# Second attention on one core: the order of product kinds alternates from step to step on TensorE, ScalarE and VectorE, and opening banks are exchanged

## The chip, the cores and the metric

The kernel runs on one core of a Trainium2 chip. The metric is the device time of one execution in microseconds; lower is better. The kernel before takes 1789.56 us, the median of three runs (1787.97 to 1791.72).

The core's engines are named as the profile names them: PE is TensorE (matmuls; PEld its weight loads), DVE is VectorE, ACT is ScalarE, POOL is GpSimd, SP is SyncE, which issues the transfers. Each works through its own list of instructions in order, and they wait for each other by semaphores.

## What is computed

Two transformer blocks for one sequence of 512 tokens and width 1024, all in float32. The first has a feed-forward layer, a Fourier mixer with latent attention, and another feed-forward layer. The second block has an attention of two kinds and a feed-forward layer. The change lies in the attention of the second block:

```python
NSA_HEADS = 8
NSA_KV = 2
DSA_HEADS = 8
DSA_TOPK = 256
...
o_nsa = nsa_attention(...)   # compressed, selected and windowed branches, gated by g
    o = g[..., 0:1] * o_cmp + g[..., 1:2] * o_slc + g[..., 2:3] * o_win
...
o_dsa = dsa_attention(...)   # keys chosen by an index score
        _, sel = lax.top_k(score, k_top)
        s = jnp.einsum('bqhd,bqkd->bhqk', qg, kg) * scale
        p = masked_softmax(s, mask)
...
        o = jnp.concatenate([o_nsa, o_dsa], axis=-1) @ w_out[l]
```

With 512 tokens the selected and the windowed branch see all earlier keys, so each of the 8 NSA heads has two causal softmaxes over up to 512 keys (one with the keys `ks`, one with `kw`) beside a small one over the compressed keys. The 8 DSA heads have one each, over keys `kd`, with a mask made from the 128 best index scores of a row.

## The kernel before

The order of all work is written out by hand, engine by engine; every wait is a semaphore. Activations lie transposed (features on partitions, 512 tokens along the free axis). Weights come in through `raw`, GpSimd splits each into a high and a low part, and three float32r products make one float32 product (`mm3`, lines 768 to 770). These products fill most of the span.

The second attention stands between the projections and the output product. Its work is cut into 12 pairs of heads, `PAIRS`: 8 for the NSA branches (for each of four head numbers one with `ks` and one with `kw`, two heads side by side) and 4 for DSA. A pair has 4 steps, one for each 128 queries; step s of a pair (s % 4 = 0 to 3) has 128, 256, 384 or 512 keys, since later keys are masked. Of each step, on each engine:

- TensorE, `pair_scores(s)` (line 1378): two score products of 64 rows each, side by side on the array, into two of the four banks `B_S2`. It waits until VectorE has read the scores of step s - 2 (`at_nm`).
- VectorE, `pair_maxima` (line 2529): adds the mask to the scores in PSUM, writes them to `p2` and takes the row maximum, `at_nm`.
- ScalarE, `pair_exp` (line 1895): the exponential with its row sum, in place, `at_exp`.
- VectorE, `pair_inverse(s)` (line 2537), one step later: the reciprocal of two row sums, `pr_inv`.
- GpSimd, `scale_probabilities` (line 745): times the reciprocal (and the gate), `pr_p`. In the first steps pieces of two weight splits stand between.
- TensorE, `pair_transposes(s)` (line 1389), `LAG_T` = 3 steps after the scores: 1 to 4 blocks of 128 x 128 for each of two heads, into the two banks `B_T2`. A transpose waits until its bank was copied out (`at_ev`).
- ScalarE, `pair_turn` (line 1890): copies the turned blocks from PSUM to `pt2`, `at_ev`.
- TensorE, `pair_values` (line 1409), `LAG_V` = 7 steps after the scores: the products with the values, step j of a pair with 512 - 128 j columns, side by side for two heads, into a bank of `B_O`. The first of a pair waits for the copies of the whole pair:

```python
            if j == 0:
                pe.wait_ge(at_ev, PAIR_T0 + 8 * pi + 8)
```

For every second NSA pair two products of the compressed branch (`compressed_values`, line 1394) stand ahead of them. Where a chunk of the output ends, ScalarE copies it out (line 1902) and VectorE takes the low part (line 2552). On VectorE `select(1)` stands beside steps 4 to 31 (three steps of four): one round of the choice of the best index scores (lines 2408 and 2409).

In each step TensorE has scores, transposes, values in this order; ScalarE has the copies of step s - 3 and then the exponentials of step s; VectorE has the maxima first. Ahead of step 1 TensorE turns the probabilities of the compressed branch (`turn_compressed`, line 1421), into banks 4 and 6, and waits until ScalarE has copied them to `ptc` (line 1882), since bank 4 is also one of the scores'. `rotate2(13)`, the last rotation of the queries `qd`, is done by VectorE in step 1 (lines 2260 to 2263) from data which ScalarE copies (`raw_copy(13)`).

Of the kernel before, what the change touches and what calls it, by code (L numbers as in the profile page):

```python
# [16 lines left out]
F32 = mybir.dt.float32  # L17
# [6 lines left out]
P = 128  # L24
D = 1024
T = 512
# [112 lines left out]
def build(nc, a, out):  # L139
# [514 lines left out]
    MLA_STEPS = 2 * MLA_HEADS  # L654
    LAG_T1, LAG_V1 = 2, 3
    B_S, B_T, B_O = (0, 1, 2, 4), (3, 5), (6, 7)
    B_S2, B_T2 = (1, 5, 4, 0), (2, 3)
    def turned1(t):

        return (sq, tt)[t // 2 % 2][:, t % 2]  # L660
# [105 lines left out]
    def _(pe):  # L766
# [605 lines left out]
        def pair_scores(s):  # L1372
            for t in (2 * s, 2 * s + 1):
                if t >= 4:
                    pe.wait_ge(at_nm, PAIR_T0 + t - 3)
            w = P * (s % 4 + 1)
            for side, x in enumerate(PAIRS[s // 4]):
                pe.matmul(ps[:, B_S2[(2 * s + side) % 4], 0:w], x["q"](s % 4), x["k"](w),  # L1378
                          start=True, stop=True).then_inc(at_s, 1)

        def pair_transposes(s):
            for t in (2 * s, 2 * s + 1):
                pe.wait_ge(pr_p, t + 1)
                if t < 2:
                    pe.wait_ge(rp_out, ROT1 + 14)
                else:
                    pe.wait_ge(at_ev, PAIR_T0 + t - 1)
                for c in range(s % 4 + 1):
                    last = pe.transpose(ps[:, B_T2[t % 2], P * c:P * c + P], p2[:, (t + 4) % P_SLOTS, P * c:P * c + P], ident)  # L1389
                last.then_inc(at_tr, 1)  # L1390

        def compressed_values(c):
            for g in range(NSA_KV):
                pe.matmul(ps[HD * g:HD * g + HD, B_O[c % 2]], v_diag[:, g, c, :], ptc[:, g, :], start=True, stop=False)

        def pair_values(pi, j):

            c = chunk_of(pi)
            if j == 0:
                pe.wait_ge(at_ev, PAIR_T0 + 8 * pi + 8)  # L1400
                if pi >= 8 or pi % 2 == 0:
                    if c >= 2:
                        pe.wait_ge(o_lo_done, PAIR_C0 + c - 1)
                    if pi == 0:
                        pe.wait_ge(cm_kv_ev, 2)
                    if pi < 8:
                        compressed_values(c)
            for side, x in enumerate(PAIRS[pi]):
                last = pe.matmul(ps[HD * side:HD * side + HD, B_O[c % 2], P * j:T], x["v"](j),  # L1409
                                 turned(8 * pi + side)(PT_ROW * j + P * j, T - P * j),  # L1410
                                 start=pi >= 8 and j == 0, stop=chunk_ends(pi) and j == 3)
            if j == 3:
                last.then_inc(pr_pv, 1)

        def turn_compressed():
            pe.wait_ge(cm_sub, 2)
            for b in range(2):
                pe.wait_ge(cm_p, b + 1)
                for gr in range(2):
                    for q in range(2):  # L1420
                        last = pe.transpose(ps[:, 4 + 2 * b, P * (2 * gr + q):P * (2 * gr + q) + P],
                                            cs[:, b, P * (2 * q + gr):P * (2 * q + gr) + P], ident)
                last.then_inc(cm_tr, 1)

        pe.wait_ge(rp_rot, ROT1 + 13)
        pe.wait_ge(cm_hid_ev, 2)
        for s in range(PAIR_STEPS + LAG_V + 1):
            if s == 1:
                turn_compressed()
                pe.wait_ge(cm_ev, 2)  # L1430
                pe.wait_ge(rp_rot, ROT1 + 14)
            if s == 32:
                pe.wait_ge(kd_up, 1)
            if s < PAIR_STEPS:
                pair_scores(s)
            if LAG_T <= s < PAIR_STEPS + LAG_T:
                pair_transposes(s - LAG_T)
            pi, j = values_at(s)
            if pi is not None:
                pair_values(pi, j)  # L1440

        pe.wait_ge(o_lo_done, 12)
        for i in range(8):
# [137 lines left out]
    def _(act):  # L1581
# [295 lines left out]
            act.activation(cs[:, b], cs[:, b], ACT.Exp, scale=HD ** -0.5).then_inc(cm_exp, 1)  # L1877
        raw_copy(12)
        raw_copy(13)
        for b in range(2):  # L1880
            act.wait_ge(cm_tr, b + 1)
            act.copy(ptc[:, :, 2 * P * b:2 * P * b + 2 * P],
                     ps[:, 4 + 2 * b].rearrange("p (g q) -> p g q", g=2)).then_inc(cm_ev, 1)
# [13 lines left out]

        for s in range(PAIR_STEPS + LAG_V + 1):
            c = finished_at(s)
            if c is not None:  # L1900
                act.wait_ge(pr_pv, (s - LAG_V) // 4)
                act.copy(h_hi[:, c], ps[:, B_O[c % 2]]).then_inc(o_hi_done, 1)
            for t in (2 * (s - LAG_T), 2 * (s - LAG_T) + 1):
                if 0 <= t < 2 * PAIR_STEPS:
                    pair_turn(t)
            for t in (2 * s, 2 * s + 1):
                if t < 2 * PAIR_STEPS:
                    pair_exp(t)

        root_table(act)  # L1910
        norm_squares(act, 4, y_ready, 0, y2)
# [20 lines left out]
    def _(dve):  # L1932
# [600 lines left out]
        def pair_inverse(s):  # L2533
# [2 lines left out]
            c = 2 * s % 16  # L2536
            dve.reciprocal(small2[:, 32 + c:34 + c], small2[:, 16 + c:18 + c]).then_inc(pr_inv, 1)

        rotate2(12, qd[:, 2])
        values_diagonal()  # L2540
        for s in range(PAIR_STEPS + LAG_V + 1):
            for t in (2 * s, 2 * s + 1):
                if t < 2 * PAIR_STEPS:
                    pair_maxima(t)
            if 1 <= s <= PAIR_STEPS:
                pair_inverse(s - 1)
            if s == 1:
                rotate2(13, qd[:, 3])
            c = finished_at(s)
            if c is not None:  # L2550
                dve.wait_ge(o_hi_done, PAIR_C0 + c + 1)
                dve.tensor_tensor(h_lo[:, c], ps[:, B_O[c % 2]], h_hi[:, c].bitcast(F32), ALU.subtract).then_inc(o_lo_done, 1)  # L2552
            if 4 <= s < 32 and s % 4 < 3:
                select(1)

        step(dve.tensor_tensor(postmix2, fac[:, A_POSTMIX:A_POSTMIX + 8], fac[:, A_POSTMIX:A_POSTMIX + 8], ALU.mult))
        def out2(m):
# [139 lines left out]
```

## Time and profile before

| | us |
|---|---|
| median of three runs | 1789.56 |
| lowest and highest run | 1787.97, 1791.72 |
| the profiled execution, its own time | 1787.86 |
| its span in the trace | 1786.1 |
| TensorE busy in the span | 1763.6 (99%) |
| GpSimd, VectorE, ScalarE busy | 1181.0 (66%), 974.3 (55%), 382.4 (21%) |
| the second attention, first score product to first output product | 1248.1 to 1363.6 |
| TensorE busy in these 115.6 us | 109.4 |
| VectorE, ScalarE, GpSimd busy in them | 83.3, 95.9, 69.4 |

The span is what the trace shows of one execution; the time of the execution is 1.8 us longer. Busy shares are means over the stretch. PEclk is the granted clock of TensorE as a share of the full 2.4 GHz; 0.50 is the lower level of 1.2 GHz. A row's idle time is the engine's time without work just before it, with the instruction that ended it.

### The profile page before, as it was taken

The page shows a single profiled execution, that of the slowest core. Times are in us where ns is not written, and L with a number is a line of the kernel's source. Part 1 is how long each engine was busy: PE and PEld are TensorE (multiplying, and loading weights), DVE is VectorE, ACT ScalarE, POOL GpSimd, SP SyncE. Part 2 cuts the span into 40 slices and gives each one's busy share as a digit, 9 for nine tenths or more (in the row PEclk, how much of TensorE's full clock was granted, in tenths as well). Part 3 has the DMA queues.
Part 4 walks back from the last instruction along what each step waited for, and adds up shares of the span by engine and source line. Part 5 has one row for each costly group of instructions (what it writes and reads, how often), then busy time and mean ns, then how long its engine had stood idle before and what let it go on. Part 6 is the DMA issues. An engine that isn't in the chain of part 4 may idle for free.

```text
span 1786.1 us, 24918 instructions
## 1 busy us (share of the span) xinstructions
PE 1763.6 (99%) x8821; PEld 1394.4 (78%) x8821; DVE 974.3 (55%) x1664; ACT 382.4 (21%) x827; POOL 1181.0 (66%) x1182
## 2 busy tenths in 40 slices
PE   8999999999999999999999999999999999999998
PEld 6888888887876788888888888878446778888887
DVE  4855345544655105565514556799874887007613
ACT  3111000012246211211100001455884110000001
POOL 4676767675665477677677768755754677668862
PEclk9999999999999999999999999999999999999999
DMA  9655465542330132455435543513000322333221
GB/s 355 215 189 176 141 206 186 161 153 66 100 99 25 36 107 94 142 171 188 125 110 191 188 127 94 127 50 95 25 25 1 95 71 96 114 96 93 95 94 48
DMA packets 245549, 212.93 MB, mean 119 GB/s; under 512 B 45986, under 2 KB 240991, under 8 KB 245471
## 3 DMA queue, kind: packets, MB, share of 16 engines
q1 hardware_dynamic: 229440, 211.18, 37.0%
q10 hardware_dynamic: 16030, 0.72, 0.5%
q8 instruction: 48, 0.79, 0.2%
q14 instruction: 31, 0.25, 0.0%
HBM read 209.72 MB, written 2.10 MB: 119 GB/s over the span
## 4 chain that ended last, share of the span: by engine, by line
PE 70%; POOL 13%; issue 9%; DVE 5%; DMA 1%; ACT 1%; ACTq 0%; POOLq 0%; DVEq 0%
PE ps L768 19%; PE ps L770 18%; PE ps L769 18%; POOL w_lo L697 8%; POOL w_hi L692 2%; PE ps L1378 2%; POOL w_hi L691 2%; PE ps L1389 2%; PE ps L1149 2%; PE ps L1409 2%; DMA raw<-in_ffn_w_down 1%; PE ps L1170 1%; PE ps L1158 1%; PE ps L809 1%; DVE tt L2260 0%
## 5 line engine op out<-in xcount | busy, mean ns | idle before, releaser
L697 POOL TENSOR_TENSOR w_lo<-raw,w_hi 128x512 fp32r<-128x512 f32 (+4 forms) x576 | 736.3, 1307 | 11.8
L768 PE MATMUL ps<-h_hi,w_hi 128*128 128x512 f32 x1192 | 467.8, 392 | 1.8 <-DVE h_lo L2552 1.4
L770 PE MATMUL ps<-h_hi,w_lo 128*128 128x512 f32 x1192 | 464.8, 390 | 0.0
L769 PE MATMUL ps<-h_lo,w_hi 128*128 128x512 f32 x1192 | 464.6, 390 | 0.0
L689 POOL TENSOR_TENSOR w_hi<-raw,ones 128x8 fp32r<-128x8 f32 x144 | 33.3, 232 | 449.5 <-PE ps L770 385.3
L768 PEld LDWEIGHTS ps<-h_hi,w_hi 128*128 128x128 f32 x1192 | 223.9, 188 | 54.4 <-issue 5.9
L770 PEld LDWEIGHTS ps<-h_hi,w_lo 128*128 128x128 f32 x1192 | 223.9, 188 | 47.3
L769 PEld LDWEIGHTS ps<-h_lo,w_hi 128*128 128x128 f32 x1192 | 224.0, 188 | 46.2
L768 PE MATMUL ps<-g_hi,w_hi 128*128 128x512 f32 x608 | 237.7, 391 | 0.1
L770 PE MATMUL ps<-g_hi,w_lo 128*128 128x512 f32 x608 | 236.6, 389 | 0.0
L769 PE MATMUL ps<-g_lo,w_hi 128*128 128x512 f32 x608 | 236.6, 389 | 0.0
L2012 DVE SCALAR_TENSOR_TENSOR ps<-ada,cT,ps 128x256 f32<-128x256 f32 x312 | 152.8, 490 | 11.0
L692 POOL TENSOR_SCALAR w_hi<-raw 128x1024 fp32r<-128x1024 f32 (+3 forms) x144 | 158.0, 1097 | 0.0
L691 POOL TENSOR_SCALAR w_hi<-raw 128x1016 fp32r<-128x1016 f32 (+3 forms) x144 | 140.7, 977 | 0.0
L768 PEld LDWEIGHTS ps<-g_hi,w_hi 128*128 128x128 f32 x608 | 114.1, 188 | 25.9 <-issue 1.6
L770 PEld LDWEIGHTS ps<-g_hi,w_lo 128*128 128x128 f32 x608 | 114.1, 188 | 23.9
L769 PEld LDWEIGHTS ps<-g_lo,w_hi 128*128 128x128 f32 x608 | 114.2, 188 | 23.3
L2098 DVE TENSOR_TENSOR tt<-sg,ps 128x512 f32<-128x512 f32 x44 | 30.3, 688 | 173.7 <-PE ps L770 170.7
L2069 DVE SCALAR_TENSOR_TENSOR xT<-ps,fac,xT 128x512 f32<-128x512 f32 x32 | 24.0, 750 | 126.1 <-PE ps L770 126.1
L1620 ACT COPY rb<-ps 128x128 f32<-128x128 f32 x26 | 7.0, 267 | 280.5 <-PE ps L883 280.5
L1922 ACT ACTIVATE sg<-ps 128x512 f32<-128x512 f32 x32 | 17.4, 596 | 228.2 <-PE ps L770 213.7
L2100 DVE TENSOR_TENSOR g_lo<-tt,g_hi 128x512 f32 x44 | 61.8, 1405 | 5.4
(408 smaller groups left out, 2405.6 us busy)
## 6 DMA issues: line engine op xcount, KB each, us to landing
ada<-in_ada_w SPq DMA_DIRECT2D x31, 1024.0 KB, 7.0
ada<-in_w_ada SPq DMA_DIRECT2D x24, 1024.0 KB, 7.2
raw<-in_ffn_w_gate SPq DMA_DIRECT2D x22, 1024.0 KB, 5.3
raw<-in_ffn_w_up SPq DMA_DIRECT2D x22, 1024.0 KB, 5.2
raw<-in_w_in SPq DMA_DIRECT2D x16, 1024.0 KB, 5.1
raw<-in_w_up SPq DMA_DIRECT2D x16, 1024.0 KB, 5.3
raw<-in_w_down SPq DMA_DIRECT2D x16, 1024.0 KB, 4.8
raw<-in_ffn_w_down SPq DMA_DIRECT2D x16, 768.0 KB, 4.8
```

What stands on the lines that cost most here:

```text
L691: pool.tensor_scalar(hi[:, 8:half], src[:, 8:half], 1.0, 1.0, ALU.mult, ALU.mult)
L692: pool.tensor_scalar(hi[:, half:size], src[:, half:size], 1.0, 1.0, ALU.mult, ALU.mult).then_inc(hi_done, 1)
L697: last = pool.tensor_tensor(lo[:, c], src[:, c], hi[:, c].bitcast(F32), ALU.subtract)
L768: pe.matmul(o, wh, xh, start=start, stop=False)
L769: pe.matmul(o, wh, xl, start=False, stop=False)
L770: return pe.matmul(o, wl, xh, start=False, stop=stop)
L1149: pe.matmul(ps[:, B_S[t % len(B_S)]], q_all[:, h, P * qc:P * qc + P], k_all[:, h], start=True, stop=True).then_inc(at_s, 1)
L1378: pe.matmul(ps[:, B_S2[(2 * s + side) % 4], 0:w], x["q"](s % 4), x["k"](w), start=True, stop=True).then_inc(at_s, 1)
L1389: last = pe.transpose(ps[:, B_T2[t % 2], P * c:P * c + P], p2[:, (t + 4) % P_SLOTS, P * c:P * c + P], ident)
L1409: last = pe.matmul(ps[HD * side:HD * side + HD, B_O[c % 2], P * j:T], x["v"](j), turned(8 * pi + side)(PT_ROW * j + P * j, T - P * j), sta ...
L2012: ins = dve.scalar_tensor_tensor(dst if j == NC - 1 else running, w[:, j], cT[:, c, j:j + 1], running, ALU.mult, ALU.add)
L2100: dve.tensor_tensor(g_lo[:, bass.ds(k, 1)], tt[:, m:m + 1], g_hi[:, bass.ds(k, 1)].bitcast(F32), ALU.subtract).then_inc(f["hid"], 1)
```

## The change

Everything that changes lies in the second attention.

- TensorE: even steps keep the order scores, transposes, values; odd steps have values, transposes, scores. So two steps run S T V, V T S, and the next begins with S again.
- ScalarE: even steps have the two exponentials first and then the two copies of step s - 3; odd steps keep copies first.
- VectorE: even steps have the maxima first, as before; in odd steps they come last, behind the reciprocal, the last rotation (step 1), the low part of the output and the selection round.
- Banks: the fourth score bank is 7 in place of 0, the output banks are 6 and 0 in place of 6 and 7, and the turned compressed probabilities lie in banks 6 and 3 in place of 4 and 6.
- The opening: TensorE no longer waits for `ptc` and for the last raw copy before the scores of step 1, but for the compressed values to be read out of bank 7 (`cm_kv_ev`), and, ahead of the turns, for rotation 12 (bank 3). The wait for `ptc` moves to the second transpose, which uses bank 3. ScalarE copies `ptc` after the exponentials of step 0.

The diff, cut to its core (`scores_step` and its like call what stood in the loop before, `step_maxima` calls `pair_maxima` twice, `compressed_turned` is the copy of `ptc`; the products and copies that name `B_O` now name `B_O2`, those of the compressed turns `B_CT`):

```diff
-    B_S2, B_T2 = (1, 5, 4, 0), (2, 3)
+    B_S2, B_T2, B_O2, B_CT = (1, 5, 4, 7), (2, 3), (6, 0), (6, 3)
...
         def pair_transposes(s):
             for t in (2 * s, 2 * s + 1):
                 pe.wait_ge(pr_p, t + 1)
-                if t < 2:
+                if t == 0:
                     pe.wait_ge(rp_out, ROT1 + 14)
+                elif t == 1:
+                    pe.wait_ge(cm_ev, 2)
                 else:
                     pe.wait_ge(at_ev, PAIR_T0 + t - 1)
...
         def turn_compressed():
             pe.wait_ge(cm_sub, 2)
+            pe.wait_ge(rp_out, ROT1 + 13)
...
             if s == 1:
                 turn_compressed()
-                pe.wait_ge(cm_ev, 2)
-                pe.wait_ge(rp_rot, ROT1 + 14)
+                pe.wait_ge(cm_kv_ev, 2)
             if s == 32:
                 pe.wait_ge(kd_up, 1)
-            if s < PAIR_STEPS:
-                pair_scores(s)
-            if LAG_T <= s < PAIR_STEPS + LAG_T:
-                pair_transposes(s - LAG_T)
-            pi, j = values_at(s)
-            if pi is not None:
-                pair_values(pi, j)
+            if s % 2 == 0:
+                scores_step(s)
+                transposes_step(s)
+                values_step(s)
+            else:
+                values_step(s)
+                transposes_step(s)
+                scores_step(s)
...
-            for t in (2 * (s - LAG_T), 2 * (s - LAG_T) + 1):
-                if 0 <= t < 2 * PAIR_STEPS:
-                    pair_turn(t)
-            for t in (2 * s, 2 * s + 1):
-                if t < 2 * PAIR_STEPS:
-                    pair_exp(t)
+            for exponentials in (s % 2 == 0, s % 2 == 1):
+                for t in (2 * s, 2 * s + 1) if exponentials else (2 * (s - LAG_T), 2 * (s - LAG_T) + 1):
+                    if 0 <= t < 2 * PAIR_STEPS:
+                        pair_exp(t) if exponentials else pair_turn(t)
+            if s == 0:
+                for b in range(2):
+                    compressed_turned(b)
...
         for s in range(PAIR_STEPS + LAG_V + 1):
-            for t in (2 * s, 2 * s + 1):
-                if t < 2 * PAIR_STEPS:
-                    pair_maxima(t)
+            if s % 2 == 0:
+                step_maxima(s)
             if 1 <= s <= PAIR_STEPS:
                 pair_inverse(s - 1)
...
             if 4 <= s < 32 and s % 4 < 3:
                 select(1)
+            if s % 2:
+                step_maxima(s)
```

The order on ScalarE shows it best. Beside one NSA pair (p are the probabilities `p2`, pt the turned ones `pt2`, ps PSUM; the width in keys stands last) ScalarE has before, from the exponentials of a 384 step on:

```order
L1895 ACTIVATE p_107,small_134<-p_107,small_134 128x384 x2
L1902 CAST h_hi<-ps 128x512
L1890 COPY pt_108<-ps 128x128 x2
L1895 ACTIVATE p_107,small_134<-p_107,small_134 128x512 x2
L1890 COPY pt_108<-ps 128x2x128 x2
L1895 ACTIVATE p_107,small_134<-p_107,small_134 128x128 x2
L1890 COPY pt_108<-ps 128x3x128 x2
L1895 ACTIVATE p_107,small_134<-p_107,small_134 128x256 x2
L1890 COPY pt_108<-ps 128x4x128 x2
L1895 ACTIVATE p_107,small_134<-p_107,small_134 128x384 x2
```

Copies and exponentials alternate, and the copies of a step stand ahead of its exponentials. The same stretch now:

```order
L1913 ACTIVATE p_107,small_134<-p_107,small_134 128x384 x2
L1908 COPY pt_108<-ps 128x4x128 x2
L1920 CAST h_hi<-ps 128x512
L1908 COPY pt_108<-ps 128x128 x2
L1913 ACTIVATE p_107,small_134<-p_107,small_134 128x512 x2
L1913 ACTIVATE p_107,small_134<-p_107,small_134 128x128 x2
L1908 COPY pt_108<-ps 128x2x128 x2
L1908 COPY pt_108<-ps 128x3x128 x2
L1913 ACTIVATE p_107,small_134<-p_107,small_134 128x256 x2
L1913 ACTIVATE p_107,small_134<-p_107,small_134 128x384 x2
L1908 COPY pt_108<-ps 128x4x128 x2
```

Two steps' exponentials stand together, 256 and 384 wide or 512 and 128 wide, and the copies of two steps follow them.

On TensorE, one pair from its 128-column scores on, before (scores L1378, transposes L1389, values L1409, qn the queries, kst the identity):

```order
L1378 MATMUL ps<-ks,qn 128x128 x2
L1389 MATMUL ps<-kst,p_107 128x128 x4
L1409 MATMUL ps<-pt_108,v_104 64x384 x2
L1378 MATMUL ps<-ks,qn 128x256 x2
L1389 MATMUL ps<-kst,p_107 128x128 x6
L1409 MATMUL ps<-pt_108,v_104 64x256 x2
L1378 MATMUL ps<-ks,qn 128x384 x2
L1389 MATMUL ps<-kst,p_107 128x128 x8
L1409 MATMUL ps<-pt_108,v_104 64x128 x2
L1378 MATMUL ps<-ks,qn 128x512 x2
L1389 MATMUL ps<-kst,p_107 128x128 x2
L1409 MATMUL ps<-pt_108,v_104 64x512 x2
```

and now (transposes L1391, values L1411):

```order
L1378 MATMUL ps<-ks,qn 128x128 x2
L1391 MATMUL ps<-kst,p_107 128x128 x4
L1411 MATMUL ps<-pt_108,v_104 64x384 x2
L1411 MATMUL ps<-pt_108,v_104 64x256 x2
L1391 MATMUL ps<-kst,p_107 128x128 x6
L1378 MATMUL ps<-ks,qn 128x256 x2
L1378 MATMUL ps<-ks,qn 128x384 x2
L1391 MATMUL ps<-kst,p_107 128x128 x8
L1411 MATMUL ps<-pt_108,v_104 64x128 x2
L1411 MATMUL ps<-pt_108,v_104 64x512 x2
L1391 MATMUL ps<-kst,p_107 128x128 x2
L1378 MATMUL ps<-ks,qn 128x512 x2
```

The values with 128 columns, the last of a pair, are now followed at once by those with 512, the first of the next; before, scores and transposes stood between the two. Two score products follow each other in the same way.

## Rows read from the trace of the kernel before

**Rows 1.** Stretches: us, busy by engine (PE, PEld, DVE, ACT, POOL), PEclk, DMA.

```profile
1328.00:1338.00 10.00, 10.00 (x62) 4.63 (x62) 5.41 (x26) 8.79 (x30) 4.13 (x8) 1.00 0.01 2
```

**Rows 2.** Chain that ended last, one pair: start us, us, engine, tile, line.

```profile
1275.87 0.42 PE ps L1378 x4
1276.30 0.59 PE ps L1389 x4
1276.88 0.80 PE ps L1409 x4
...
1278.31 0.80 PE ps L1389 x6
...
1279.70 0.85 PE ps L1378 x4
1280.55 1.02 PE ps L1389 x8
1281.57 0.37 PE ps L1409 x4
...
1283.37 1.01 PE ps L1394 x4
1284.37 0.86 PE ps L1409 x4
1285.23 0.42 PE ps L1378 x4
```

**Rows 3.** Timeline of VectorE beside that pair: start us, us, engine, line, operation.

```profile
1275.08 0.69 DVE L2529 CUSTOM_DVE_ANT_0 p<-ps,kst 128x512 f32<-128x512 f32 x1
1275.69 0.08 DVE L2529 DVE_READ_ACCUMULATOR2_ANT small<- 128x1 f32 x1
...
1277.44 0.68 DVE L2408 MAX8 c<-score 128x8 f32<-128x512 f32 x1
...
1278.94 0.42 DVE L2529 CUSTOM_DVE_ANT_0 p<-ps,kst 128x256 f32<-128x256 f32 x1
```

**Rows 4.** Timeline of ScalarE beside the same pair.

```profile
1275.81 0.72 ACT L1895 ACTIVATE p<-p,small 128x512 f32<-128x512 f32 x1 [0.55 <-DVE small L2529]
...
1277.24 0.62 ACT L1890 COPY pt<-ps 128x256 f32<-128x256 f32 x2
1277.75 0.41 ACT L1895 ACTIVATE p<-p,small 128x128 f32<-128x128 f32 x1
...
1279.57 0.52 ACT L1895 ACTIVATE p<-p,small 128x256 f32<-128x256 f32 x1
...
1281.17 1.07 ACT L1890 COPY pt<-ps 128x512 f32<-128x512 f32 x2 [0.50 <-PE ps L1389]
1282.13 0.63 ACT L1895 ACTIVATE p<-p,small 128x384 f32<-128x384 f32 x1
```

**Rows 5.** Stretches of 1 us around the opening, and one later.

```profile
1253.00:1254.00 1.00, 1.00 (x8) 0.54 (x4) 0.48 (x3) 0.01 (x1) 0.00 (x0) 0.50 0.00 0
...
1257.00:1258.00 1.00, 0.49 (x4) 0.33 (x4) 1.00 (x6) 1.00 (x3) 0.46 (x1) 1.00 0.00 0
...
1259.00:1260.00 1.00, 1.00 (x6) 0.51 (x4) 0.14 (x3) 1.00 (x5) 1.00 (x2) 0.55 0.00 0
...
1262.00:1263.00 1.00, 1.00 (x5) 0.32 (x5) 0.97 (x6) 1.00 (x4) 1.00 (x2) 0.74 0.00 0
...
1418.00:1419.00 1.00, 0.24 (x1) 0.28 (x2) 0.90 (x2) 1.00 (x2) 0.00 (x0) 1.00 1.07 380
```

**Rows 6.** Timelines of TensorE and VectorE in the opening.

```profile
1252.27 3.90 PE L1378 MATMUL ps<-ks,qn 64*128 64x256 f32 x12 [2.62 <-ACT ptc L1882]
...
1253.52 0.42 DVE L2529 CUSTOM_DVE_ANT_0 p<-ps,kst 128x256 f32<-128x256 f32 x1 [3.00 <-PE ps L1378]
```

**Rows 7.** Timeline of TensorE at the end of the stage.

```profile
1352.45 1.13 PE L1378 MATMUL ps<-kd,qd 64*128 64x512 f32 x4
...
1363.61 0.50 PE L768 MATMUL ps<-h_hi,w_hi 128*128 128x512 f32 x1 [1.41 <-DVE h_lo L2552]
```

More of the change, by code:

```diff
@@ L1393, in compressed_values @@
             for g in range(NSA_KV):
-                pe.matmul(ps[HD * g:HD * g + HD, B_O[c % 2]], v_diag[:, g, c, :], ptc[:, g, :], start=True, stop=False)
+                pe.matmul(ps[HD * g:HD * g + HD, B_O2[c % 2]], v_diag[:, g, c, :], ptc[:, g, :], start=True, stop=False)
         def pair_values(pi, j):
@@ L1408, in pair_values @@
             for side, x in enumerate(PAIRS[pi]):
-                last = pe.matmul(ps[HD * side:HD * side + HD, B_O[c % 2], P * j:T], x["v"](j),
+                last = pe.matmul(ps[HD * side:HD * side + HD, B_O2[c % 2], P * j:T], x["v"](j),
                                  turned(8 * pi + side)(PT_ROW * j + P * j, T - P * j),
@@ L1420, in turn_compressed, with scores_step, transposes_step, values_step @@
                     for q in range(2):
-                        last = pe.transpose(ps[:, 4 + 2 * b, P * (2 * gr + q):P * (2 * gr + q) + P],
+                        last = pe.transpose(ps[:, B_CT[b], P * (2 * gr + q):P * (2 * gr + q) + P],
                                             cs[:, b, P * (2 * q + gr):P * (2 * q + gr) + P], ident)
                 last.then_inc(cm_tr, 1)
+        def scores_step(s):
+            if s < PAIR_STEPS:
+                pair_scores(s)
+        def transposes_step(s):
+            if LAG_T <= s < PAIR_STEPS + LAG_T:
+                pair_transposes(s - LAG_T)
+        def values_step(s):
+            pi, j = values_at(s)
+            if pi is not None:
+                pair_values(pi, j)
         pe.wait_ge(rp_rot, ROT1 + 13)
@@ L1879, in _, with compressed_turned @@
         raw_copy(13)
-        for b in range(2):
+        def compressed_turned(b):
             act.wait_ge(cm_tr, b + 1)
             act.copy(ptc[:, :, 2 * P * b:2 * P * b + 2 * P],
-                     ps[:, 4 + 2 * b].rearrange("p (g q) -> p g q", g=2)).then_inc(cm_ev, 1)
+                     ps[:, B_CT[b]].rearrange("p (g q) -> p g q", g=2)).then_inc(cm_ev, 1)
         def pair_turn(t):
@@ L1901, in _ @@
                 act.wait_ge(pr_pv, (s - LAG_V) // 4)
-                act.copy(h_hi[:, c], ps[:, B_O[c % 2]]).then_inc(o_hi_done, 1)
-            for t in (2 * (s - LAG_T), 2 * (s - LAG_T) + 1):
-                if 0 <= t < 2 * PAIR_STEPS:
-                    pair_turn(t)
-            for t in (2 * s, 2 * s + 1):
-                if t < 2 * PAIR_STEPS:
-                    pair_exp(t)
+                act.copy(h_hi[:, c], ps[:, B_O2[c % 2]]).then_inc(o_hi_done, 1)
+            for exponentials in (s % 2 == 0, s % 2 == 1):
[5 more added lines that the diff above has]
+                    compressed_turned(b)
         root_table(act)
@@ L2537, in pair_inverse, with step_maxima @@
             dve.reciprocal(small2[:, 32 + c:34 + c], small2[:, 16 + c:18 + c]).then_inc(pr_inv, 1)
+        def step_maxima(s):
+            for t in (2 * s, 2 * s + 1):
+                if t < 2 * PAIR_STEPS:
+                    pair_maxima(t)
         rotate2(12, qd[:, 2])
@@ L2551, in _ @@
                 dve.wait_ge(o_hi_done, PAIR_C0 + c + 1)
-                dve.tensor_tensor(h_lo[:, c], ps[:, B_O[c % 2]], h_hi[:, c].bitcast(F32), ALU.subtract).then_inc(o_lo_done, 1)
+                dve.tensor_tensor(h_lo[:, c], ps[:, B_O2[c % 2]], h_hi[:, c].bitcast(F32), ALU.subtract).then_inc(o_lo_done, 1)
             if 4 <= s < 32 and s % 4 < 3:
                 select(1)
+            if s % 2:
+                step_maxima(s)
         step(dve.tensor_tensor(postmix2, fac[:, A_POSTMIX:A_POSTMIX + 8], fac[:, A_POSTMIX:A_POSTMIX + 8], ALU.mult))
```

## The prediction

> **What bounds the kernel now.** I read the stretches of 10 us first, then the chain of work that ended last, then what VectorE and ScalarE do beside one pair of heads. The second attention has 48 steps, four to a pair, and lies from 1248.1 to 1363.6 us. In its steady part TensorE is busy 10.00 of 10.00 us at granted clock 1.00, while VectorE, ScalarE and GpSimd have idle time [rows 1]. The chain there is TensorE alone: scores S, transposes T, value products V, and S again, each starting where the last one ended [rows 2]. The pair from 1275.87 to 1285.23 takes 9.36 us with the two products of the compressed branch in it, 8.50 without their 0.86.
>
> What a change of kind costs stands in the same rows. The value product behind the compressed one, of the same kind and width, takes 0.86 us; the compressed one, behind transposes, 1.01 us: a V after another kind pays 0.15 us. Transposes of 4, 6 and 8 blocks take 0.59, 0.80 and 1.02 us, 0.107 us a block and 0.16 over. Scores of 128 and 384 columns take 0.42 and 0.85 us, 0.215 us for 128 columns and 0.21 over. A step so pays 0.15 + 0.16 + 0.21 = 0.52 us for its three changes.
>
> **The change part by part.** *Fewer changes of kind.* Two steps now run S T V V T S, and the next S follows: four changes where there were six, since one V and one S in two follow their own kind. That saves 0.15 + 0.21 = 0.36 us in two steps, 0.73 us a pair, 12 x 0.73 = 8.8 us over the 12 pairs if nothing else waited. The new changes, V to T and T to S, are priced by the kind that begins, as above.
>
> *Who waits now.* What decides is what moves on ScalarE. Before, each step first copied the turned blocks out (two copies) and then did its two exponentials. Now an even step does its exponentials first. ScalarE works in order, so the copies stand behind exponentials of scores that TensorE has only just finished. TensorE needs those copies: a transpose waits until the copy from its bank (two banks) is out, and the first value product of a pair waits for the pair's last copy, both on at_ev. Each happens once in a pair.
>
> First wait, counted from the end of the 256-column scores (step 4p+1). The maximum takes 0.42 us [rows 3]; ScalarE then does two exponentials of 256 (0.52 each), two of 384 (0.63 each) and only then the two copies of 512 (1.07 together) [rows 4]: 0.42 + 1.04 + 1.26 + 1.07 = 3.79. A hand-off takes some 0.05 (the maximum read out at 1275.77, its exponential from 1275.81 [rows 3, 4]); with three, 3.9 us. TensorE meanwhile has S of 384 without a change (0.85 - 0.21 = 0.64), T of 8 blocks (1.02) and V of 128 (0.37) [rows 2], 2.03 us. Next on it is the pair's first V, which needs those copies; before, S of 512 and T of 2 blocks stood in between as well (1.07 + 0.37 by the figures above). The wait is **1.9 us**.
>
> Second wait, from the end of the 512-column scores (step 4p+3): maximum 0.69 [rows 3], exponentials 2 x 0.72 and 2 x 0.41, the first of two copies of 256, 0.62 / 2 = 0.31 [rows 4], hand-offs 0.15: 3.41 us. TensorE has S of 128 (0.21 without a change), T of 4 (0.59), V of 384 (0.80) and V of 256 without a change ((0.80 - 0.15) x 2/3 = 0.43) [rows 2], 2.03 us. The transpose of 6 blocks waits **1.4 us**. A pair gains 0.73 and loses 3.3: **+2.6 us**. An earlier start helps neither chain, since the exponentials cannot begin before their scores, and those come right ahead of the work that should cover them.
>
> *VectorE's order.* Up to step 31 three steps in four hold a selection round, 1.50 us at 512 columns (1277.44 to 1278.94) [rows 3]. Two rounds now lie between the maxima of steps 4p and 4p+1. From the end of the 512 scores: 0.69, 1.44 for the exponentials that the reciprocal waits for, two rounds 3.0, two reciprocals of 0.08 and a hand-off: 5.35 us. TensorE ends its 256 scores after 2.03 + 1.4 + 0.80 + 0.64 = 4.9 us. VectorE is some 0.5 us late and the first wait grows by that: **+3.1 us** in these pairs. Six such pairs (steps 8 to 31) and three without (32 to 43): 18.6 + 7.8 = **+26.4 us**. GpSimd's scaling, 4.1 of 10 us busy [rows 1], is wanted three steps after its scores, later than the copies, and I price it at nothing; POOL's weight splits and SP's queue keep their places.
>
> *The opening.* TensorE waited 2.62 us for the copies of the compressed branch ahead of the scores of step 1, and VectorE 3.00 us for those scores [rows 6]. Other banks take that wait away. But the first transposes still need VectorE's last rotation, and it now stands ahead of the maxima of step 1. So the gain is at most 2.6 and at least 0; I take the middle, -1.3. The first pair then pays the waits like the others, +3.1. Net **+1.8 us**.
>
> *The end.* The last scores ended at 1353.6 and the output product began at 1363.61 [rows 7], 10.0 us later. V (1.01) and T of 2 (0.37) now stand ahead of those scores: with the two waits and the saving 1.4 + 3.3 - 0.7 = +4.0. They no longer lie in the tail, which gives back between 0 (ScalarE paced it) and 1.4; I take 0.8. Net **+3.2 us**.
>
> Sum at the full clock: 26.4 + 1.8 + 3.2 = **+31.4 us**. On the profiled execution's own 1787.86 us that makes 1819.3; the median of the three runs is 1.70 us higher, so 1821. The work behind the stage is bound by TensorE and moves along.
>
> **The clock.** Behind the 2.62 us wait of the opening the granted clock read 0.50. It was back at 1.00 at 1257, where TensorE had 0.49 us of work in 1 us, and fell again: 0.55 at 1259, two stretches of 0.50, 0.74 at 1262. At 1418, 0.24 us of work in 1 us left it at 1.00 [rows 5]. The new waits of 1.4 us lie near what kept the clock, those of 2.4 us near the one that lost it. A fall like that at 1259 takes 0.45 + 0.50 + 0.50 + 0.26 = 1.7 us of array time, some of it under a wait: 1.5. I take one fall in each of the six pairs with the long wait, **+9 us**, so **1830 us**. The ends: no fall (1821), and two in each pair with half of each hidden, 24 x 0.8 = 19 (1840).
>
> The Trainium skill, TensorE: Matmul & The Clock Gate, section A second HAM failure mode: psum-queue depth-cycling, tells of a kernel that goes through PSUM banks with short idle times between its groups, so that the clock swings between its levels. The fall at 1259, with no wait over 1 us before it, agrees. By that rule the 9 us belong in the sum; without it the forecast is 1821.
>
> **The rivals.** *Full clock.* The same waits and no falls: 1821. For it speaks the stretch at 1418, against it the fall at 1259.
>
> *Faster: changes of kind are saved and nothing waits.* 8.8 us and the opening's 1.3: 1780. One thing decides: the copies must be out within the 2.03 us that TensorE has from the end of its scores, where the rows give 3.9 and 3.4. It would take copies ahead of the exponentials, or exponentials of half the length. A weaker form makes VectorE the bound, whose three rounds (4.5 us) and eight maxima (0.28 to 0.69 by the two shown, 3.9) fill up to 8.4 of a pair's 8.5 us: then only pairs without selection gain, 1786 to 1789, no change that can be measured.
>
> *Smaller waits.* If neighbours on ScalarE overlap more than their rows add up to, each of the 24 waits is 0.5 to 1 us shorter: 12 to 24 us less, 1797 to 1809.
>
> *Clock low through most of the stage.* Products then take twice, the waits vanish under them, and a pair needs 2 x 7.8 = 15.5 us, 7 more, over 11 pairs: 1867. The same mix of products held 1.00 [rows 1], though without waits. The Trainium skill, same page, section Part 4: PE-mode transpose, says that transposes do not count as activity for the clock in the usual way, which would favour this rival; no row separates the kinds.
>
> *The change does not save what it says.* If V behind V still paid 0.15 and S behind S 0.21, up to 8.8 us would come back, mostly under the waits: 1830 to 1836, inside the range.
>
> **How the numbers follow.** Waits with some falls 0.46 (1826 to 1846), waits at full clock 0.33 (1812 to 1826), smaller waits 0.08, clock low 0.06, faster 0.04, no change 0.03. The forecast is the first, 1830. From 1810 to 1846 the range holds the first two, some 8 in 10. Faster and slower count from 0.2% (3.6 us, about what a measurement of this kernel can tell): faster 0.04, same 0.03, slower 0.93.
>
> **What would show it.** TensorE idle at the first V of each pair and at its transposes, released by ScalarE's copies, 1.9 to 2.4 and 1.4 us, about a dozen of each; ScalarE idle ahead of exponentials; pairs of 11 to 12.5 us; a stage of 145 to 165 us instead of 115.5; a granted clock under 1.00 in several of its stretches; V behind V and S behind S without overhead. I am wrong if TensorE stays at 10 of 10 us, or if its waits end with GpSimd's scaling.

## The result and the profile after

The changed kernel takes 1838.26 us, the median of five runs (1831.72 to 1840.64), against 1789.56 before (1787.97 to 1791.72): 1.026 times, with a 95% interval from 1.025 to 1.028. It is 48.7 us slower. The profiled execution took 1840.64 us, its span is 1838.8; that of the kernel before took 1787.86, so the two profiles lie 52.8 us apart.

The page of the profile after, the busy line of the engines and three rows of the 40 slices:

```profile
PE 1779.5 (97%) x8821; PEld 1406.0 (76%) x8821; DVE 978.5 (53%) x1664; ACT 383.7 (21%) x827; POOL 1180.2 (64%) x1182
...
PE   8999999999999999999999999997778999999998
...
ACT  2110000011256111211000013446555111000001
...
PEclk9999999999999999999999999998889999999999
```

TensorE has as many instructions as before (8821) and is busy 15.9 us longer, with 3 slices at 7 and 3 of the clock at 8. These slices lie in the second attention. It went from 1252.22 to 1416.45 us, 164.2 us where it took 115.5 before: +48.7. That this is also the difference of the two medians is chance. The 4.1 us by which the stage starts later had come up in earlier stages, which the change does not touch: in the profiles of all the kernels here it starts between 1248.1 and 1252.4 us, with the order of before as with that of after.

Stretches of 10 us (us, busy by engine PE, PEld, DVE, ACT, POOL, then PEclk), which answer to [rows 1]:

```profile
1280.00:1290.00 10.00, 7.29 (x31) 3.48 (x30) 4.89 (x17) 3.96 (x13) 4.59 (x8) 0.67 0.01 2
1300.00:1310.00 10.00, 7.15 (x50) 4.17 (x48) 7.60 (x28) 6.56 (x23) 5.46 (x9) 1.00 0.01 2
1350.00:1360.00 10.00, 7.36 (x26) 2.78 (x28) 2.71 (x10) 3.97 (x12) 2.39 (x4) 0.66 0.00 1
```

No engine is full any more. Two things have to be told apart: at 1300 the clock is whole and TensorE waits 2.85 of 10 us; at 1280 and 1350 it waits nearly as much (2.71 and 2.64) and works at 0.67 as well, with 26 to 31 products in 10 us instead of 50. The timeline of TensorE over one pair at the full clock (start, us, line, shapes; in brackets the idle time before the row and what ended it), which answers to [rows 2]:

```profile
1298.23 1.08 PE L1396 MATMUL ps<-ptc,v_diag 128*64 128x512 f32 x4 [2.27 <-ACT pt L1908]
1299.14 1.03 PE L1411 MATMUL ps<-pt,v 128*64 128x512 f32 x4
1300.10 0.44 PE L1391 MATMUL ps<-kst,p 128*128 128x128 f32 x2
1300.47 1.13 PE L1378 MATMUL ps<-kw,qn 64*128 64x512 f32 x4
1301.43 0.39 PE L1378 MATMUL ps<-ks,qn 64*128 64x128 f32 x4
1301.75 0.66 PE L1391 MATMUL ps<-kst,p 128*128 128x128 f32 x4
1302.34 1.30 PE L1411 MATMUL ps<-pt,v 128*64 128x384 f32 x8
1305.05 0.84 PE L1391 MATMUL ps<-kst,p 128*128 128x128 f32 x6 [1.42 <-POOL p L745]
1305.83 1.35 PE L1378 MATMUL ps<-ks,qn 64*128 64x256 f32 x8
1307.10 1.09 PE L1391 MATMUL ps<-kst,p 128*128 128x128 f32 x8
1308.12 0.44 PE L1411 MATMUL ps<-pt,v 128*64 128x128 f32 x4
1310.83 1.98 PE L1411 MATMUL ps<-pt,v 128*64 128x512 f32 x4 [2.26 <-ACT pt L1908]
```

From 1298.23 to 1310.83 a pair with the compressed branch takes 12.60 us, 9.36 before: +3.24. It has two waits, 1.42 us at the transpose of 6 blocks and 2.26 at the next pair's first V. Over the whole stage, the table of waits (line waited, for whom: us in total, times, longest), for TensorE and then for ScalarE:

```profile
PE ps L1411 <- ACT pt L1908: 14.6, 8, 2.7
PE ps L1391 <- POOL p L745: 10.5, 8, 2.1
PE ps L1396 <- ACT pt L1908: 8.5, 4, 2.7
PE ps L1391 <- ACT pt L1908: 4.0, 5, 1.4
PE ps L1391 <- DVE qd L2282: 3.2, 1, 3.2
...
ACT p L1913 <- DVE small L2548: 34.8, 25, 2.5
```

The first V of the 12 pairs (L1411, and L1396 where the compressed branch leads) waits 23.1 us for ScalarE's copies, the transposes (L1391) 14.5 for GpSimd or ScalarE by the profile's names. ScalarE itself waits 34.8 us ahead of its exponentials. The copies come late because of their place, as its timeline shows with two rows of GpSimd beside it:

```profile
1302.36 0.72 ACT L1913 ACTIVATE p<-p,small 128x512 f32<-128x512 f32 x1 [1.46 <-DVE small L2548]
...
1304.17 0.39 ACT L1913 ACTIVATE p<-p,small 128x128 f32<-128x128 f32 x1
...
1304.56 0.62 ACT L1908 COPY pt<-ps 128x256 f32<-128x256 f32 x2
...
1309.74 1.04 ACT L1908 COPY pt<-ps 128x512 f32<-128x512 f32 x2
```

```profile
1299.64 1.31 POOL L745 TENSOR_SCALAR p<-p,small,gsig 128x384 f32<-128x384 f32 x2
1304.18 1.52 POOL L745 TENSOR_SCALAR p<-p,small,gsig 128x512 f32<-128x512 f32 x2 [3.23 <-DVE small L2556]
```

The turned blocks of 256 lay ready in PSUM since about 1302.3, when the transposes of 4 blocks ended, but four exponentials stood ahead of their copies. The first copy is out near 1304.87, and the transposes of 6 start at 1305.05. The profile puts this wait down to GpSimd, which the prediction named as a sign of its being wrong. It is a misreading: the 6 blocks need the scaling of 384 columns, done at 1300.95; the GpSimd row that ran when the wait ended is the 512-wide one, for the step after. In the DSA pair from 1379.79 on, the same wait of the same length is put down to ScalarE:

```profile
1379.79 1.08 PE L1411 MATMUL ps<-pt,v 128*64 128x512 f32 x4 [1.75 <-ACT pt L1908]
...
1385.75 0.84 PE L1391 MATMUL ps<-kst,p 128*128 128x128 f32 x6 [1.42 <-ACT pt L1908]
...
1391.02 1.08 PE L1411 MATMUL ps<-pt,v 128*64 128x512 f32 x4 [1.75 <-ACT pt L1908]
```

That pair, without selection, takes 11.23 us, 8.50 before: +2.73.

### The profile page after: what moved, and what is told of

Same layout as the page of the kernel before. It is cut to its first block, busy times and chain, and to the rows that moved or that the text cites. A ratio compares the mean times of both kernels' runs of the same rounds, so it can differ in the third digit from the quotient of the medians.

```text
span 1838.8 us, 24930 instructions
## 1 busy us (share of the span) xinstructions
PE 1779.5 (97%) x8821; PEld 1406.0 (76%) x8821; DVE 978.5 (53%) x1664; ACT 383.7 (21%) x827; POOL 1180.2 (64%) x1182
## 4 chain that ended last, share of the span: by engine, by line
PE 67%; POOL 13%; issue 10%; DVE 5%; ACT 4%; DMA 1%; ACTq 0%; POOLq 0%; DVEq 0%
PE ps L768 18%; PE ps L769 18%; PE ps L770 18%; POOL w_lo L697 8%; ACT p L1913 2%; POOL w_hi L692 2%; POOL w_hi L691 2%; PE ps L1149 2%; PE ps L1378 1%; PE ps L1391 1%; PE ps L1411 1%; PE ps L1170 1%; DMA raw<-in_ffn_w_down 1%; PE ps L1158 1%; PE ps L809 1%
## 5 line engine op out<-in xcount | busy, mean ns | idle before, releaser
L745 POOL TENSOR_SCALAR p<-p,small,gsig 128x128 f32<-128x128 f32 (+3 forms) x64 | 38.6, 613 | 73.5 <-DVE small L2556 73.3
```

The lines of the kernel that those rows point to most:

```text
L745: pool.tensor_scalar(p, p, by, 1.0 if x["gate"] is None else x["gate"](qc), ALU.mult, ALU.mult).then_inc(pr_p, 1)
```

## Experiments

Each edit is against the changed kernel unless another is named. Three causes stood against each other for the waits: ScalarE's copies behind exponentials, VectorE's maxima at the end of odd steps, and GpSimd's scaling, which the profile names. Beside them stood the question how much of the loss is the clock.

**ScalarE's copies first again, all else as changed.**

```diff
-            for exponentials in (s % 2 == 0, s % 2 == 1):
+            for exponentials in (False, True):
```

> The changed kernel, but ScalarE does the two copies ahead of the two exponentials in every step, as before; all else as changed. Theory A (the copies stand behind two steps' exponentials): the wait at a pair's first value product loses the two 384-wide exponentials (about 1.25 us), the wait at the 6-block transposes the two 128-wide ones (0.8 us), some 2 us in each of 12 pairs, 24 us, and several falls of the clock go with them: 1798 to 1810 us. Theory B (VectorE's later maxima) or C (TensorE's order alone, whatever ScalarE does): no change, 1832 to 1841 us.

1812.23 us (1810.39 to 1814.65), 1.0125 [1.0109, 1.0142] (the ratio to the kernel before and its 95% interval): one line of order on ScalarE takes back 26 of the 48.7 us. Its timeline of TensorE at the same two places of a DSA pair, and at the first V of a pair beside selection:

```profile
1303.72 1.74 PE L1411 MATMUL ps<-pt,v 128*64 128x512 f32 x4 [1.84 <-ACT pt L1908]
...
1355.11 0.85 PE L1391 MATMUL ps<-kst,p 128*128 128x128 f32 x6 [0.65 <-ACT pt L1908]
...
1359.19 1.08 PE L1411 MATMUL ps<-pt,v 128*64 128x512 f32 x4 [0.57 <-ACT pt L1908]
```

In the DSA pairs 1.75 became 0.57 and 1.42 became 0.65, and in the table of waits GpSimd's scaling no longer appears (`L1391 <- ACT pt` 8.8 us in 13 waits), though nothing on GpSimd was changed. In the six pairs beside selection the transposes wait 0.65 or less too, but the first V still waits 1.84 (2.3 in two of them) where it waited 2.27 (2.7): not 1.25 us less, as expected, but 0.43. ScalarE's timeline shows why, at the exponentials of 256 of such a pair and of a DSA pair:

```profile
1301.62 0.51 ACT L1913 ACTIVATE p<-p,small 128x256 f32<-128x256 f32 x1 [1.61 <-DVE small L2548]
...
1357.09 0.51 ACT L1913 ACTIVATE p<-p,small 128x256 f32<-128x256 f32 x1 [0.33 <-DVE small L2548]
```

The 1.28 us between these two rows is the 1.27 between the waits of 1.84 and 0.57. Beside selection VectorE does two rounds ahead of the maxima of 256, and TensorE, which now waits 0.77 us less at its transposes, comes to its scores that much earlier: the half microsecond by which VectorE was late before and these 0.77 make the 1.27. So once the copies stand first, VectorE holds the first wait of these pairs. What stays elsewhere, 0.57 and 0.65, fits the exponentials of the neighbouring step, which the alternated order of TensorE still puts between two groups of copies; no run takes that part out at this parity. The time is 2 us above the range for this cause: the waits that did not shrink are some 5 us (0.82 in six pairs).

The clock came part of the way back. Counting each 1 us stretch of the stage by how far its granted clock lay below 1.00 (0.50 counts 1 us), the changed kernel has 47.8 us at the low clock, this one 20.5, the kernel before 6.8. Behind the opening it falls three times here, each time behind a wait of 1.84 or 2.3 us, and never behind those of 0.57 and 0.65. All waits of TensorE in the stage add up to 28.9 us instead of 42.5, so of the 26 us some 13.6 are waits; the rest goes with the 27.3 us less at the low clock.

**Maxima first in every step, all else as changed.**

```diff
-            if s % 2 == 0:
-                step_maxima(s)
+            step_maxima(s)
...
-            if s % 2:
-                step_maxima(s)
```

> The changed kernel, but VectorE has the maxima first in every step, as before. Theory B (VectorE's order): most of the loss goes, under 1810 us. Theory A: the chain through ScalarE stays, and selection rounds and reciprocals now stand no better: 1832 to 1848 us.

1844.33 us (1840.15 to 1845.81), 1.0299 [1.0282, 1.0316]: 6 us slower still. So with the exponentials first, VectorE's order is not what costs the time; to put its maxima first makes the first wait longer. From the table of waits, and ScalarE's exponential of 384 beside selection:

```profile
PE ps L1411 <- ACT pt L1908: 17.2, 8, 3.3
PE ps L1396 <- ACT pt L1908: 13.6, 4, 3.7
```

```profile
1313.40 0.61 ACT L1913 ACTIVATE p<-p,small 128x384 f32<-128x384 f32 x1 [1.31 <-DVE small L2548]
```

The exponentials of 384, which the copies stand behind, now wait 1.31 us themselves, since a selection round has come between the maxima of 256 and of 384. Copies first and maxima first together, at this parity, was not run.

**Only the banks and the opening, all three orders as before.**

```diff
-            if s % 2 == 0:
+            if True:
                 scores_step(s)
...
-            for exponentials in (s % 2 == 0, s % 2 == 1):
+            for exponentials in (False, True):
...
-            if s % 2 == 0:
-                step_maxima(s)
+            step_maxima(s)
...
-            if s % 2:
-                step_maxima(s)
```

> Only the exchanged banks and the opening of the changed kernel; the three engines keep the order of before in every step. Theories A, B and C agree: the stage is not longer than before, the opening 0 to 2.6 us shorter, 1786 to 1790 us. If the banks or the opening were the cause of the loss: over 1800 us.

1788.25 us (1786.56 to 1789.59), 0.9991 [0.9981, 1.0000], 1.3 us below the kernel before, at the edge of what can be told. The wait of 2.62 for `ptc` [rows 6] is gone, and one for the last rotation has taken its place:

```profile
PE ps L1391 <- DVE qd L2282: 1.9, 1, 1.9
```

**Filled waits.** Products of 128 columns that nobody reads, into the output bank that is idle, six ahead of each pair's first V and four ahead of its transposes of 6 blocks. They cannot make a wait shorter; they keep TensorE at work in it.

```diff
+        def fill(pi, n, own):
...
+            for _ in range(n):
+                pe.matmul(ps[:, B_O2[(c + (not own)) % 2], 0:P], ident, ident, start=True, stop=True)
...
         def pair_transposes(s):
+            if s % 4 == 2 and s >= 4:
+                fill(s // 4 - 1, 4, False)
...
             if j == 0:
+                fill(pi, 6, pi >= 8 or pi % 2 == 0)
                 pe.wait_ge(at_ev, PAIR_T0 + 8 * pi + 8)
```

> The changed kernel with unused products of 128 columns put on TensorE right ahead of the two waits of each pair: six (1.3 us) before the first value product, four (0.85 us) before the 6-block transposes, into an output bank that holds nothing at that time. They are shorter than the waits at the full clock, so they add nothing to the chain. If the falls of the clock cost 10 to 16 us: the granted clock stays at 1.00 in most of the stage and the time is 1820 to 1828 us. If they cost nothing, since the waits absorb them: 1832 to 1841 us.

1826.41 us (1824.83 to 1827.83), 1.0204 [1.0187, 1.0221]: 12 us faster than the changed kernel, with more work on TensorE. Stretches of the opening and of the later stage, and the first V of a pair with its filler:

```profile
1260.00:1270.00 10.00, 7.75 (x38) 5.53 (x35) 7.20 (x29) 7.07 (x25) 7.41 (x13) 0.54 0.00 1
...
1300.00:1310.00 10.00, 8.94 (x62) 5.75 (x60) 7.19 (x27) 7.07 (x24) 7.10 (x10) 1.00 0.00 1
1350.00:1360.00 10.00, 9.45 (x66) 6.27 (x64) 2.89 (x13) 6.26 (x22) 4.29 (x8) 1.00 0.01 2
```

```profile
1305.90 1.60 PE L1389 MATMUL ps<-kst 128*128 128x128 f32 x12
1308.23 1.08 PE L1424 MATMUL ps<-pt,v 128*64 128x512 f32 x4 [0.73 <-ACT pt L1921]
```

The filler (1.53 us and a rest of 0.73) takes the place of the wait of 2.26, and the clock reads 1.00 from 1270 on. Low clock remains in the opening alone, 10.2 us by the count above. The stage takes 152.0 us, 12.2 less. At the very end six fillers come where TensorE had waited 0.36 us only, which costs about 1.1, so the clock was worth some 13.3 us for 37.6 us at the low level, 0.35 us for each: part of a slower stretch lies under waits that would have been there anyway. The changed kernel's own trace shows that too: where the products just ahead of it ran at the low clock, the wait of 1.42 us is only 0.51 to 0.86.

**The changed kernel without the selection rounds.**

```diff
-            if 4 <= s < 32 and s % 4 < 3:
-                select(1)
```

> The changed kernel without the 21 selection rounds of steps 4 to 31 (left out; the mask of the last heads is then incomplete). If selection on VectorE lengthens the waits: the first wait of a pair falls from about 2.25 to 1.75 us and the 6-block transposes wait for ScalarE's copies instead of GpSimd's scaling, 3 to 9 us less in all with the falls of the clock, 1829 to 1835 us. If the copies behind the exponentials are all there is: 1836 to 1840 us.

1821.98 us (1821.91 to 1826.19), 1.0177 [1.0161, 1.0192]: 16.3 us less than the changed kernel, where I had expected 3 to 9. From TensorE's timeline:

```profile
1300.63 0.85 PE L1391 MATMUL ps<-kst,p 128*128 128x128 f32 x6 [1.42 <-POOL p L745]
...
1305.90 1.08 PE L1411 MATMUL ps<-pt,v 128*64 128x512 f32 x4 [1.76 <-ACT pt L1908]
```

The first wait is now 1.76 where it was 2.26, as without selection in the DSA pairs. In two of the six pairs it had been 2.7; there VectorE ends a set of rounds with one more instruction (L2431, 0.68 and 0.43 us). The waits of all first V add up to 19.0 us instead of 23.1, 4.1 less. The low clock fell from 47.8 to 23.9 us, at 0.35 another 8.4. The sum of 12.5 is close to what the stage of the two profiles shows, 152.2 against 164.2. Of the other 4 us of the medians, 2.4 lie ahead of the stage, which starts at 1249.77 and 1252.22 in these two executions, and the rest is the distance of each median from its profiled execution. I had also expected that ScalarE would be named at the wait of 1.42; GpSimd still is, with the same length, so this run does not settle the name. The copies-first run does.

**The kernel before without the selection rounds** (the same two lines taken out of it).

> The kernel before without the same 21 selection rounds (left out). VectorE is not on the chain of the kernel before, so all theories expect no change: 1787 to 1791 us. It is the ground that the run without selection is compared with.

1789.49 us (1787.12 to 1792.11), 0.9997 [0.9988, 1.0006]. Before the change selection costs nothing that can be measured, but the room on VectorE is small beside it, as a stretch of the kernel before shows:

```profile
1278.00:1288.00 10.00, 10.00 (x64) 4.80 (x61) 9.62 (x34) 8.49 (x29) 9.04 (x14) 1.00 0.36 105
```

**The other parity.** If copies have to be out within what TensorE does between its scores and the place that needs them, the alternation can start on the other foot: odd steps S T V, even ones V T S. Then the scores of 384 and 512 and a transpose of 2 blocks lie between the last copies of a pair and its first V. ScalarE keeps copies first, VectorE maxima first.

```diff
-            if s % 2 == 0:
+            if s % 2:
                 scores_step(s)
...
-            for exponentials in (s % 2 == 0, s % 2 == 1):
+            for exponentials in (False, True):
...
-            if s % 2 == 0:
-                step_maxima(s)
+            step_maxima(s)
...
-            if s % 2:
-                step_maxima(s)
```

> The orders alternate on TensorE as in the change but with odd and even exchanged (even steps values, transposes, scores; odd steps scores, transposes, values), ScalarE copies first and VectorE has the maxima first in every step; banks and opening as changed. A pair's last transposes are then followed by two score products and another transpose before its first values, some 2.2 us that the copies have, and one step's exponentials stand ahead of copies. If saved changes of kind are real and only the waits ate them: no waits of over 0.5 us in the steady part, 8.5 us a pair down to 7.8 without selection (four pairs, 3 us), less where VectorE's selection bounds the pair, and 1.3 us of the opening: 1783 to 1787 us. If alternation itself costs (theory C): over 1795 us.

1786.56 us (1785.79 to 1788.75), 0.9983 [0.9974, 0.9992]. With the last rotation of the queries ahead of the reciprocal in step 1 as well:

> The same, and VectorE does the last rotation ahead of the first reciprocal, which waits for ScalarE; the first transposes need that rotation. Expected 0.5 to 1 us less than the same without it, 1782 to 1786.5 us; if the rotation waits for the raw copy alone and not for the reciprocal, no change.

1785.96 us (1785.16 to 1789.40), 0.9981 [0.9972, 0.9990]. The two can't be told apart; both are faster than the kernel before, by some 3 us or 0.2%, and by some 52 us than the changed one. Of 8.8 us saved on changes of kind and 1.3 in the opening about a third arrives. Against the changed kernel three things differ here, the parity, ScalarE's order and VectorE's; against the copies-first run still two, so how much is the parity's alone is not shown. Stretches of the second of them, one beside selection and one in the DSA pairs:

```profile
1300.00:1310.00 10.00, 9.87 (x64) 4.91 (x60) 9.45 (x34) 8.35 (x27) 6.67 (x11) 1.00 0.36 105
...
1330.00:1340.00 10.00, 9.77 (x71) 5.55 (x69) 5.77 (x30) 9.32 (x34) 5.40 (x11) 1.00 0.01 2
```

VectorE is at 9.45 of 10 us beside selection, ScalarE at 9.32 in the DSA pairs. Two NSA pairs, one with the compressed branch and one without, take 17.6 to 18.4 us from transposes of 6 blocks to transposes of 6 blocks, 17.9 before, with waits of up to 0.64 us for VectorE's maxima; the DSA pairs take 7.8 to 8.1, 8.5 before. So beside selection nothing is gained. To see which of them holds the rest, this version without selection:

> The run with odd and even exchanged and the rotation first, without the 21 selection rounds of steps 4 to 31 (left out; the mask of the last heads is then incomplete). It asks what ate the rest of the 8.8 us of changes of kind, of which that run gave back some 2 to 3 beside the opening. If VectorE's selection alone held the pairs back: 12 pairs at 7.8 us in place of 8.5, 1778 to 1781 us. If ScalarE (7.0 to 7.5 us of exponentials and copies a pair, in order) holds them at some 8.1 us as in the four pairs that have no selection: 1782 to 1785 us.

1782.84 us (1782.08 to 1785.39), 0.9964 [0.9951, 0.9978], 3.1 us less than with selection, where the same omission gave nothing in the kernel before. From TensorE's timeline, an NSA pair from its transposes of 6 blocks to the next pair's, and the same place in a DSA pair:

```profile
1302.21 0.87 PE L1391 MATMUL ps<-kst,p 128*128 128x128 f32 x6
...
1304.85 1.77 PE L1378 MATMUL ps<-ks,qn 64*128 64x384 f32 x8
...
1310.02 0.87 PE L1391 MATMUL ps<-kst,p 128*128 128x128 f32 x6
...
1334.58 0.85 PE L1391 MATMUL ps<-kst,p 128*128 128x128 f32 x6 [0.23 <-ACT pt L1908]
```

7.81 us without any wait, 8.50 before: the changes of kind give 0.69 a pair, priced at 0.73. The DSA pairs but the first stay at 8.1, with a wait of 0.23 us for ScalarE's copies, so VectorE holds one part of the gain and ScalarE another, the case of 1782 to 1785 in the expectation.

## Why the prediction was right, and where its terms were off

1830 was forecast, within 1810 to 1846; 1838.26 came. Step by step:

- **Changes of kind: right.** V of 128 and 512, S of 512 and 128, S of 256 and 384 follow each other without overhead. In the DSA pair the two S from 1381.17 take 1.28 us together, 1.49 before (0.42 by [rows 2] and the 1.07 of the prediction). The unwaited pair of the last run shows 0.69 against 0.73. So that rival (the change does not save what it says) is out.
- **The two waits: right in place, size and cause.** First V: 1.75 without selection (1.9 forecast), 2.26 with (2.4; the longest 2.7). Transpose of 6 blocks: 1.42 (1.4). The copies-first run shows the cause, for the transposes in all pairs and for the first V in those without selection. Adding up an in-order queue's rows, without any overlap between neighbours, was enough; the rival of smaller waits is out. One clause of the faster rival was wrong, though: copies ahead of the exponentials are not sufficient for it, as 0.57 and 0.65 us of wait remain, and 1.84 beside selection. What that rival needed came with the other parity, together with maxima first, and there its weaker form, VectorE as the bound at 1786 to 1789, is near what was measured (1785.96 and 1786.56).
- **VectorE's half microsecond: right directly, incomplete.** 0.5 us of the first wait hangs on selection, as forecast. The term does not say that the low clock costs more than the waits themselves (8.4 against 4.1 us), nor that VectorE's lateness stands ready behind ScalarE's copies and is 1.27 us as soon as these come early. That VectorE has idle time holds for the stretch of [rows 1], which lies in the DSA pairs; beside selection it is at 9.62 of 10 us.
- **The pair: right.** +2.73 without selection (2.6), +3.24 with (3.1).
- **The sum at the full clock: some 4 us short.** It can be read from the filled run, since its clock is whole outside the opening: 152.0 - 1.1 - 115.5 = +35.4 against +31.4. From the scores of step 8 to those of step 47 it takes 117.9 us, before 85.1: +32.8, forecast 26.4 + 4.0 = +30.4. Most of these 2.4 us are the six pairs beside selection, +20.4 where 18.6 stood: four at +3.24, and +3.70 in the two that hold VectorE's additional instruction. The tail, the 1.1 taken off, came out at -0.55 (-0.8). The opening, to the scores of step 8, takes 22.3 us in the changed kernel instead of 19.2: +3.1 where +1.8 stood. Its bank exchange gives 1.3 alone, the figure forecast, but that figure was only the middle between 0 and 2.6, so the match is luck; with the new orders it is lost again, since the transposes wait 3.15 us for the last rotation and not 1.9.

```profile
1258.41 0.43 PE L1391 MATMUL ps<-kst,p 128*128 128x128 f32 x2 [3.15 <-DVE qd L2282]
...
1264.44 1.52 PE L1391 MATMUL ps<-kst,p 128*128 128x128 f32 x6 [2.14 <-POOL p L745]
```

- **The clock: the term that was mis-sized.** Eight falls behind the opening's instead of six, the longest (1283 to 1291, 1351 to 1359) some 8 us. They come behind five of the six long waits (2.26 to 2.72; the one at 1298 kept the clock) and behind three of the four waits of 1.75 us, in pairs without selection. They cost 13.3 us in the filled run's measure, 9 forecast, 19 as the upper end. The changed kernel's five runs bear this out: the two at 1831.72 and 1833.08 us have a mean granted clock of 0.990, the three at 1838.26 to 1840.64 have 0.984 or 0.985. By an estimate from these figures that is some 20 us more at the low level for 6.7 us of time, a third of a microsecond for each, and the scatter of this kernel is mostly its clock. The rival at full clock, with 0.33 the strongest, fell. Clock low through most of the stage fell as well: 47.8 of 164.2 us. The Trainium skill, TensorE: Matmul & The Clock Gate, section A second HAM failure mode: psum-queue depth-cycling, describes, for a bf16 kernel, a swing between the two levels with short idle times between groups of products. The runs here agree with it, with eight falls behind waits of 1.75 to 2.72 us.
- **GpSimd at nothing: right in these pairs, though the profile names it.** The sign I had set (waits that end with GpSimd's scaling) came up in 8 rows and was a false one in the seven behind the opening. The eighth, the 2.14 us of the opening, where weight splits stand on GpSimd, is 1.19 in the copies-first run and put down to ScalarE there, so 0.95 of it hung on ScalarE's order; what held the rest is open.

The account closes: TensorE's waits in the stage add up to 42.5 us (the five rows of the table in the first section and two of 1.4 and 0.3), 6.1 before, +36.4; less 8.8 for the kinds, plus half of the 41 us more at the low clock, 20.5, makes +48.1 against +48.7. The clock is worth 13.3 and not 20.5, because at the full clock the waits are longer by a part of what the products then save.

## What to carry to other kernels

When one engine's order is alternated to save its own switching cost, walk the in-order queue of the engine that feeds it: here one swapped line on ScalarE, which is no busier for it (383.7 us, 382.4 before), cost 26 us because copies that TensorE needs stood behind exponentials whose scores had only just been made. Once that queue is in order, look for the engine that is late behind it: here VectorE, beside selection. The parity of an alternation is a choice of its own; with the larger products between hand-off and use, and the orders of ScalarE and VectorE as before, the same saving was 0.2% faster instead of 2.6% slower. Where a wait of about 2 us recurs on TensorE, price the clock beside it.

## What the runs showed of the hardware

- Products that nobody reads, put into waits of 1.4 to 2.7 us, kept the granted clock at 1.00 behind the opening and took 12 us off the time.
- Waits of 1.75 to 2.72 us ahead of the first V went with a fall of the granted clock in eight of ten pairs of the changed kernel. In the copies-first run waits of 1.84 to 2.3 us did so in three of six pairs, and waits of 0.57 and 0.65 us in none.
- A change of product kind on TensorE costs 0.15 to 0.21 us in this kernel, also with the new neighbours, and nothing where the same kind follows (7.81 us for a pair without waits, 8.50 before).
- A wait for several semaphores can be put down to an engine that has long delivered: GpSimd was named where its item was 4.1 us old, with an item of the next step that was running as the wait ended.
